# DeltaNet projections in pairs by seven products over half the contraction, first convolution tap on ScalarE

## The chip, the cores and the metric

The kernel runs on one core of a Trainium2 chip. The metric is the device time of one execution in microseconds (us), from the first to the last instruction of the program.

## What is computed

The kernel is a trunk of two layers (DEPTH = 2) over one sequence of 1024 tokens with 1024 channels, all in float32. Each layer normalises its input, projects it by one wide matrix w_in (1024 x 9232), runs two token mixers on the result, a retention with 4 heads and a gated DeltaNet with 8 heads, merges them and adds the layer's output to its input. Of the DeltaNet, which the change is about, this is what has to come out:

```
h = rmsnorm(x, norm_g)
proj = h @ w_in
(rq, rk, rv, rz, dq, dk, dv, dz, db, da, gr, gd) = jnp.split(proj, _split_points(), axis=-1)
qkv = jax.nn.silu(causal_conv(jnp.concatenate([dq, dk, dv], axis=-1), conv_w))   # 4 taps per channel
...
# per head and chunk: a triangular solve, then a recurrence over the chunks
v_new = u_n - w_n @ state
o = q_n @ state + attn_n @ v_new
state = state * exp(gl) + k_n^T @ v_new
...
o_d = rmsnorm(o) * dn_g * silu(dz)
y = sigmoid(gr) * (o_r @ w_up_r) + sigmoid(gd) * (o_d @ w_up_d)
```

## The kernel before

TensorE works in transposed form: a block is 128 columns of w_in (one head's k, q, v or z, or 128 channels of a gate), its result is 128 channels by 1024 tokens, kept as two halves of 512 tokens. A float32 product is made of three products of rounded parts: hi and lo parts of the weights (`w_hi`, `w_lo`) and of the normed input (`act_hi`, `act_lo`, 8 contraction tiles of 128 channels each). `dense_pieces` (L852) yields after every three matmuls (L866, L868, L870); such a **piece** is one contraction tile of one half, so that a block takes 16 pieces and a head's six blocks (K, Z, Q, V and the two gates D and R, of the next head) take 96.

```
eng.matmul(dense_ps[:, to, :], w_hi[:, slot, k, :], hi[:, k, seg], start=(k == 0), stop=False)
eng.matmul(dense_ps[:, to, :], w_hi[:, slot, k, :], lo[:, k, seg], start=False, stop=False)
mm = eng.matmul(dense_ps[:, to, :], w_lo[:, slot, k, :], hi[:, k, seg], start=False, stop=(k == KT - 1))
```

A weight block is loaded by SyncE (`load_w`), rounded to `w_hi` by ScalarE (`split_hi`, 128x1024, L1429) and its rest made by GpSimd as `w_lo` (L2579).

The DeltaNet of a head is cut into an **even** unit (first 512 tokens) and an **odd** unit (last 512 tokens). `unit_schedule(kind)` (L123) is one list of steps for a unit, in 24 slots, and every engine walks this same list in `delta_unit`, does its own part of each step, and waits on semaphores where it needs another engine's. In an even or odd unit each slot is followed by two pieces ("fill"), so 48 pieces fill the gaps of a unit. Each engine takes its steps strictly in order. There is one unit "first" ahead, seven even and seven odd ones in turn, then "even_last" and "odd_last", in each of two layers. The steps that matter below, with their line on each engine (PE is TensorE, DVE VectorE, ACT ScalarE, POOL GpSimd):
- **evac**: ACT copies a finished half block out of PSUM (L1419), which frees the bank for the block after.
- **conv**: four taps on DVE, the first a scaling (L1970), three of multiply-add (L1973), all SBUF to SBUF. **tanh** on ACT (L1435) and **silu** on DVE (L1987) follow.
- **solve**: 15 steps of two small dependent operations on DVE (L2280, L2283), SBUF to SBUF. **spread** (L2290) ends the solve; PE's **level_v 0** (L1141) waits for it. Then **turn 0** (L2237) and the copy L2251 on DVE.
- **ks, xu, so**, once for each of four chunks: PE multiplies the state (ks, L1171), DVE makes u (L2299), PE xu (L1182) waits for u, ACT copies it, PE so (L1195, L1201, L1202), DVE makes the next state (L2314).
- **kt, vs, qt, kq, qe, mask, dec**: transposes, decays and norms, with POOL's squares (L2672), masks (L2659, L2661) and powers (L2666, L2676).
- **z_silu** (L2149): DVE takes the block Z out of PSUM.

## Time and profile before

| | |
|---|---|
| device time, median of 3 runs | 2644.19 us (2643.35 to 2647.51) |
| span of the profiled execution | 2644.2 us |
| PE busy, of the span | 99% (14874 matmuls) |
| DVE busy | 67%; 7 or 8 tenths in the slices of the DeltaNet units |
| ACT busy | 27% |
| POOL busy | 30% |
| granted TensorE clock | 0.999 of full speed |

The profile gives each engine's busy time, the span in slices, the groups of instructions, who waited for whom, and a timeline. For PE an instruction's modelled duration is longer than the distance from one matmul's start to the next, so the price of a matmul is read from starts. The seven pairs of even and odd units of the first layer lie between about 98 and 734 us, those of the second between about 1406 and 2042 us. The profiled execution's span is the device time of one of the runs to 0.1 us, so nothing has to be added around it.

### The profile page before, as it was taken

How to read it: one execution, taken by the hardware profiler on the slowest of the kernel's cores; microseconds unless marked ns; L12 is line 12 of the kernel's file. 1: busy time of each engine (PE TensorE's matmuls, PEld its weight loads, DVE VectorE, ACT ScalarE, POOL GpSimd, SP SyncE). 2: the span in 40 equal slices, each digit the busy share in tenths (PEclk: the TensorE clock that was granted, in tenths of full speed). 3: DMA queues.
4: the chain of work that ended last, by engine and by line, in shares of the span. 5: the costliest groups of instructions: out<-in, count | busy, mean ns of one | idle time of the engine just before them, and what ended most of it. 6: DMA issues, size and time to landing. Idle time of an engine off the chain costs nothing.

```text
span 2644.2 us, 40210 instructions
## 1 busy us (share of the span) xinstructions
PE 2620.6 (99%) x14874; PEld 2238.1 (85%) x14874; DVE 1761.1 (67%) x3972; ACT 704.5 (27%) x1440; POOL 798.6 (30%) x451
## 2 busy tenths in 40 slices
PE   8999999999999999999999999999999999999998
PEld 6888888888888899888877888888888998898887
DVE  7878777877755555434577778777877555653333
ACT  5333333333311212200143333333332221231001
POOL 3123333333312212334512233332322122132453
PEclk9999999999999999999999999999999999999999
DMA  5321222122211112433533222222222111133344
GB/s 174 100 85 58 81 69 85 53 86 65 85 50 43 41 35 76 130 96 120 157 90 88 77 74 69 73 77 72 67 77 73 43 51 43 41 106 100 99 135 152
DMA packets 293416, 217.79 MB, mean 82 GB/s; under 512 B 31747, under 2 KB 246101, under 8 KB 292965
## 3 DMA queue, kind: packets, MB, share of 16 engines
q1 hardware_dynamic: 259620, 159.07, 20.9%
q10 hardware_dynamic: 33600, 56.15, 6.3%
q8 instruction: 119, 1.95, 0.3%
q14 instruction: 77, 0.62, 0.1%
HBM read 176.30 MB, written 38.86 MB: 81 GB/s over the span
## 4 chain that ended last, share of the span: by engine, by line
PE 92%; DVE 3%; DMA 2%; issue 1%; ACT 1%; SPq 0%; POOL 0%; ACTq 0%; DVEq 0%; POOLq 0%
PE dense_ps L866 23%; PE dense_ps L870 23%; PE dense_ps L868 23%; PE work L849 3%; PE dense_ps L890 2%; PE dense_ps L891 2%; PE dense_ps L892 2%; PE work L1145 1%; PE work L1182 1%; PE work L1202 1%; PE work L1121 1%; PE work L1104 1%; PE work L1171 1%; PE work L1195 1%; PE work L1156 1%
## 5 line engine op out<-in xcount | busy, mean ns | idle before, releaser
L866 PE MATMUL dense_ps<-act_hi,w_hi 128*128 128x512 f32 x2552 | 1048.3, 411 | 1.7 <-DVE w_lo L1797 0.8
L870 PE MATMUL dense_ps<-act_hi,w_lo 128*128 128x512 f32 x2552 | 998.4, 391 | 0.0
L868 PE MATMUL dense_ps<-act_lo,w_hi 128*128 128x512 f32 x2552 | 997.3, 391 | 0.0
L2579 POOL TENSOR_TENSOR w_lo<-w_raw,w_hi 128x1024 fp32r<-128x1024 f32 x162 | 400.1, 2470 | 1024.5 <-ACT w_hi L1429 582.7
L870 PEld LDWEIGHTS dense_ps<-act_hi,w_lo 128*128 128x128 f32 x2552 | 479.0, 188 | 105.8
L866 PEld LDWEIGHTS dense_ps<-act_hi,w_hi 128*128 128x128 f32 x2552 | 481.0, 188 | 86.9 <-POOL act_lo L2600 2.3
L868 PEld LDWEIGHTS dense_ps<-act_lo,w_hi 128*128 128x128 f32 x2552 | 481.5, 189 | 78.8 <-issue 0.5
L1973 DVE SCALAR_TENSOR_TENSOR arena<-arena,cols 128x512 f32<-128x512 f32 x288 | 244.3, 848 | 6.1
L1429 ACT ACTIVATE w_hi<-w_raw 128x1024 fp32r<-128x1024 f32 x94 | 99.1, 1054 | 330.5 <-PE dense_ps L870 310.5
L1419 ACT ACTIVATE arena<-dense_ps 128x512 f32<-128x512 f32 x96 | 57.2, 596 | 258.5 <-PE dense_ps L870 258.5
L849 PE MATMUL work<-mk,arena 128*128 128x128 f32 x768 | 112.1, 275 | 7.9 <-DMA arena<-in_x 7.9
L2280 DVE TENSOR_TENSOR arena<-arena 128x60 f32<-128x60 f32 (+14 forms) x480 | 99.9, 208 | 20.2 <-DMA arena<-l_scratch 7.8
L892 PE MATMUL dense_ps<-v_later_lo,act_hi 128*128 128x256 f32 x384 | 107.9, 281 | 0.0
L890 PE MATMUL dense_ps<-v_later_hi,act_hi 128*128 128x256 f32 x384 | 107.9, 281 | 0.0
L891 PE MATMUL dense_ps<-v_later_hi,act_lo 128*128 128x256 f32 x384 | 107.9, 281 | 0.0
L849 PEld LDWEIGHTS work<-mk,arena 128*128 128x128 f32 x768 | 91.8, 142 | 17.7 <-issue 5.2
L2283 DVE TENSOR_TENSOR arena<-arena 128x60 f32<-128x60 f32 (+14 forms) x480 | 92.4, 192 | 16.5
L2666 POOL TENSOR_TENSOR arena<-arena,negh 128x4 f32<-128x4 f32 x32 | 33.0, 1032 | 230.1 <-DVE arena L2180 230.1
L866 PE MATMUL dense_ps<-o_hi,w_hi 128*128 128x512 f32 x256 | 99.6, 389 | 0.0
L868 PE MATMUL dense_ps<-o_lo,w_hi 128*128 128x512 f32 x256 | 99.6, 389 | 0.0
L870 PE MATMUL dense_ps<-o_hi,w_lo 128*128 128x512 f32 x256 | 99.6, 389 | 0.0
L1620 ACT ACTIVATE arena<-work 128x128 f32<-128x128 f32 x128 | 34.9, 273 | 229.7 <-PE work L1182 224.4
(262 smaller groups left out, 4094.7 us busy)
## 6 DMA issues: line engine op xcount, KB each, us to landing
w_raw<-in_w_in SPq DMA_DIRECT2D x138, 512.0 KB, 3.8
arena<-l_scratch SPq DMA_DIRECT2D x64, 256.0 KB
arena<-gate_scratch ACTq DMA_DIRECT2D x64, 256.0 KB, 2.7
gate_scratch<-arena ACTq DMA_DIRECT2D x36, 256.0 KB, 2.0
w_raw<-in_w_out SPq DMA_DIRECT2D x18, 512.0 KB, 3.7
o_scratch<-arena ACTq DMA_DIRECT2D x32, 256.0 KB, 2.2
w_raw<-in_w_up_dn SPq DMA_DIRECT2D x16, 512.0 KB, 3.6
arena<-o_scratch ACTq DMA_DIRECT2D x32, 256.0 KB, 3.7
```

The lines of the kernel that those rows point to most:

```text
L849: mm = eng.transpose(wk[bank][:, c * P:(c + 1) * P], src, ident)
L866: eng.matmul(dense_ps[:, to, :], w_hi[:, slot, k, :], hi[:, k, seg], start=(k == 0), stop=False)
L868: eng.matmul(dense_ps[:, to, :], w_hi[:, slot, k, :], lo[:, k, seg], start=False, stop=False)
L870: mm = eng.matmul(dense_ps[:, to, :], w_lo[:, slot, k, :], hi[:, k, seg], start=False, stop=(k == KT - 1))
L890: eng.matmul(dst, act_hi[:, k, tok], hi[:, k, :], start=(k == 0), stop=False)
L891: eng.matmul(dst, act_lo[:, k, tok], hi[:, k, :], start=False, stop=False)
L892: mm = eng.matmul(dst, act_hi[:, k, tok], lo[:, k, :], start=False, stop=(k == KT - 1))
L1429: eng.activation(w_hi[:, slot, :, :], w_raw[:, :, :], ACT.Copy).then_inc(w_hi_ok.sem, 1)
L1973: eng.scalar_tensor_tensor(out=acc[:, i % 2, :], in0=src, scalar=wcol, in1=acc[:, i % 2, :], op0=ALU.mult, op1=ALU.add).then_inc(conv_s.se ...
L2280: eng.tensor_tensor(xm[:, :, 0:left], column, xs[:, :, k:k + 1].to_broadcast([P, CPH, left]), ALU.mult).then_inc(sv_s.sem, 1)
L2283: eng.tensor_tensor(xs[:, :, k + 1:BASE], xs[:, :, k + 1:BASE], xm[:, :, 0:left], ALU.add)\
L2579: eng.tensor_tensor(w_lo[:, slot, :, :], w_from[second][:, :, :], w_hi[:, slot, :, :].bitcast(F32), ALU.subtract)\
```

## The change

In the even and odd units the six blocks of a head become three **pairs**: K with Z, Q with V, D with R. The contraction tiles 0 to 3 of a pair (the "thin" part: two tiles low, two tiles high, two blocks, two token halves) are a 2 x 2 by 2 x 2 block product and are made by Strassen's scheme in Winograd's form, with seven products of two tiles instead of eight. The tiles 4 to 7 ("J1", "J2") stay as they were. A pair takes 30 pieces instead of 32, and a unit 45 instead of 48.

The seven products need sums of weights (`S1` to `S4`: four GpSimd additions of 128x256 for each pair), nine rounded parts for each pair (ScalarE `part`, seven of 128x256 and two of 128x512, with a GpSimd rest for each), sums of the activations over token halves (`mix`, once in each layer in the unit "first", 14 steps, mostly GpSimd operations of 128x1024), and intermediate results that are carried between three PSUM banks (`p1`, `u3`) or parked in SBUF (`p5`, `u2`) by ScalarE copies. The second token halves of both blocks (`c12`, `c22`) are finished by a VectorE addition from PSUM. The third PSUM bank is `work5`; the products of `level_x` move to `work4`. ScalarE takes the first convolution tap. One product of each pair starts a bank that the pair before has just left: `S1` waits for `c21` to be taken, `S2` for ScalarE's copy of `p1`, and that for `c22` of the pair before.

The late tokens of two activation tiles are replaced by their mix in place; they are stored to DRAM first and loaded back before the unit "even_last". Several semaphores are merged, which changes no order.

```diff
+PARTS = ("X11", "S1", "S2", "X12", "J1", "S3", "S4", "X22", "J2")
+PART_AT = (-14, -12, -9, -6, -3, 3, 5, 7, 10)
+PAIR_PIECES = 30
+UNIT_PIECES = 45
...
+        events = {"p1": 2, "p5": 10 if u % 3 == 1 else 4, "u2": 6, "c11": 12, "u3": 14, "c12": 20, "c21": 26, "c22": 30}
...
+        if paired and waiting and waiting[0][0] == "conv" and waiting[0][2] == 0:
+            out.append(waiting.pop(0))
...
-        for _ in range(2):
+        while paired and pieces < UNIT_PIECES * (n + 1) // len(slots):
+            out.append(("fill", 1))
+            pieces += 1
...
-        elif kind in ("even", "odd"):
-            spread(0 if 3 <= n < 8 or (12 if kind == "even" else 13) <= n < 17 else 2 if n in (12, 17) or n > 17 else 1)
+        elif kind == "even":
+            spread(0 if 3 <= n < 8 or 12 <= n < 17 else 2 if n >= 17 else 1)
+        elif kind == "odd":
+            spread(0 if 3 <= n < 8 or 13 <= n < 17 else 2 if n >= 17 or n in (8, 9, 12) else 1)
...
+                        eng.wait_ge(c12_ok.sem, c12_ok.after(t - 1, 1))
+                        yield from product(t, u, a, "X11", tokens(low_k, early), True, "p1")
...
+                        eng.wait_ge(c21_ok.sem, c21_ok.after(t, 0))
+                        yield from product(t, u, c, "S1", mixed(1), True, "p5")
+                        eng.wait_ge(pc_ok.sem, pc_ok.after(t, COPIES["p1"]))
+                        yield from product(t, u, b, "S2", mixed(2), False, "p6")
+                        yield from product(t, u, a, "X12", tokens(high_k, early))
+                        yield from product(t, u, a, "J1", tokens(rest, early), False, "c11")
+                        eng.wait_ge(pc_ok.sem, pc_ok.after(t, COPIES["u2"]))
+                        yield from product(t, u, b, "S3", mixed(3), False, "p7")
+                        yield from product(t, u, c, "S4", tokens(high_k, late))
+                        yield from product(t, u, c, "J1", tokens(rest, late), False, "c12")
...
+                        eng.wait_ge(pc_ok.sem, pc_ok.after(t, COPIES["u3"]))
+                        yield from product(t, u, b, "X22", mixed(4), False, "p4")
+                        yield from product(t, u, b, "J2", tokens(rest, early), False, "c21")
+                        yield from product(t, u, a, "J2", tokens(rest, late), False, "c22")
...
+                            eng.activation(part_place(part, u, w_hi), part_from[part], ACT.Copy).then_inc(wp_hi.sem, 1)
...
+                        elif what == "conv" and kind in ("even", "odd") and step[2] == 0:
...
+                            eng.activation(acc[:, i % 2, :], raw[:, (i // 2) % 2, i % 2 * HALF:(i % 2 + 1) * HALF], ACT.Copy,
+                                           scale=cols[:, wcol:wcol + 1]).then_inc(conv_s.sem, 1)
...
+                        elif what == "pair" and step[1] in ("c12", "c22"):
...
+                            ins = eng.tensor_tensor(into, of, into, ALU.add)
...
+                            if part == "X11":
+                                eng.wait_ge(wx_in.sem, wx_in.after(w, 32))
+                                eng.tensor_tensor(w_s, raw_x["X21"], raw_x["X22"], ALU.add).then_inc(wp_lo.sem, 1)
+                                eng.wait_ge(wp_lo.sem, wp_lo.after(w, LOWS["sum_S1"]))
+                                eng.tensor_tensor(raw_x["X21"], raw_x["X11"], raw_x["X21"], ALU.subtract).then_inc(wp_lo.sem, 1)
```

What this makes of the order shows at three places. The first is VectorE in an odd unit, from the last solve step to u of the last chunk. Before:

```order
L2283 TENSOR_TENSOR arena<-arena 128x4
L2314 SCALAR_TENSOR_TENSOR arena<-arena,work 128x128
L2290 TENSOR_TENSOR arena<-arena,mk 128x512
L1973 SCALAR_TENSOR_TENSOR arena<-arena,cols 128x512
L2237 STREAM_TRANSPOSE arena<-arena 32x4x32 x4
L2251 TENSOR_TENSOR arena<-work,mk 64x256
L2299 SCALAR_TENSOR_TENSOR arena<-work,arena 128x128
```

And now (L2629 is the solve step, L2468 the addition of c22, L2660 the state, L2636 spread, L2289 a tap, L2645 u):

```order
L2629 TENSOR_TENSOR arena<-arena 128x4
L2468 TENSOR_TENSOR arena<-work,arena 128x512
L2660 SCALAR_TENSOR_TENSOR arena<-arena,work 128x128
L2636 TENSOR_TENSOR arena<-arena,mk 128x512
L2289 SCALAR_TENSOR_TENSOR arena<-arena,cols 128x512 x2
L2583 STREAM_TRANSPOSE arena<-arena 32x4x32 x4
L2597 TENSOR_TENSOR arena<-work,mk 64x256
L2645 SCALAR_TENSOR_TENSOR arena<-work,arena 128x128
```

One addition stands ahead of the spread, and two taps instead of one between spread and u. PE reaches level_v 0 (L1351, L1141 before) one piece after "so" (L1405 to L1412) there, where it had two:

```order
L1405 MATMUL work<-arena 128x128
L1411 MATMUL work<-arena 128x128
L1412 MATMUL work<-arena 128x128
L1218 MATMUL dense_ps<-act_hi,w_hi 128x512
L1219 MATMUL dense_ps<-act_lo,w_hi 128x512
L1220 MATMUL dense_ps<-act_hi,w_lo 128x512
L1351 MATMUL work<-arena 66x64 x4
```

The second place is VectorE from the end of an even unit into the odd one. Before, the last tap pair of the third convolution and its silu stood like this ahead of u of chunk 0 (L2299):

```order
L1970 TENSOR_SCALAR arena<-arena,cols 128x512
L1973 SCALAR_TENSOR_TENSOR arena<-arena,cols 128x512
L1987 SCALAR_TENSOR_TENSOR arena<-arena 128x512
L1973 SCALAR_TENSOR_TENSOR arena<-arena,cols 128x512 x2
L1987 SCALAR_TENSOR_TENSOR arena<-arena 128x512
L2299 SCALAR_TENSOR_TENSOR arena<-work,arena 128x128
```

Now three taps (L2289) stand straight ahead of u (L2645), and the silu (L2303) behind it:

```order
L2573 TENSOR_TENSOR arena<-work,arena 128x512
L2303 SCALAR_TENSOR_TENSOR arena<-arena 128x512
L2289 SCALAR_TENSOR_TENSOR arena<-arena,cols 128x512 x3
L2645 SCALAR_TENSOR_TENSOR arena<-work,arena 128x128
L2303 SCALAR_TENSOR_TENSOR arena<-arena 128x512
```

Their input is `c11` of the pair that started at piece 30 of the even unit: PE finishes it after piece 42 of 45, ScalarE copies it out and makes the first tap, and PE's xu of chunk 0 follows piece 1 of the odd unit (it followed piece 2).

The third place is GpSimd. Before, over one unit:

```order
L2579 TENSOR_TENSOR w_lo<-w_raw,w_hi 128x1024 x2
L2672 TENSOR_TENSOR arena<-arena 128x512
L2579 TENSOR_TENSOR w_lo<-w_raw,w_hi 128x1024
L2659 TENSOR_TENSOR arena<-mk,arena 128x512
L2661 TENSOR_TENSOR arena<-arena,mk 128x512
```

And now, over an odd unit, from the sums of the next pair to J1's rest:

```order
L3051 TENSOR_TENSOR arena<-w_raw 128x256
L3053 TENSOR_TENSOR w_raw<-w_raw 128x256
L3055 TENSOR_TENSOR w_lo<-w_raw,w_hi 128x256
L3060 TENSOR_TENSOR w_raw<-arena,w_raw 128x256
L3055 TENSOR_TENSOR w_lo<-arena,w_hi 128x256
L3055 TENSOR_TENSOR w_lo<-w_raw,w_hi 128x256
L3085 TENSOR_TENSOR arena<-arena 128x512
L3055 TENSOR_TENSOR w_lo<-w_raw,w_hi 128x256
L3064 TENSOR_TENSOR w_raw<-w_raw 128x256
L3055 TENSOR_TENSOR w_lo<-arena,w_hi 128x512
```

The six operations of 128x1024 of a head have become 33 of 128x256 and six of 128x512, and the squares (L3085, L2672 before) and several of the small ones stand at steps that lie inside the solve.

## Rows read from the trace of the kernel before

**Rows 1.** The page: busy time of each engine.

```profile
PE 2620.6 (99%) x14874; PEld 2238.1 (85%) x14874; DVE 1761.1 (67%) x3972; ACT 704.5 (27%) x1440; POOL 798.6 (30%) x451
```

**Rows 2.** Windows: us, busy (instructions) of PE, PEld, DVE, ACT, POOL, clock, DMA, GB/s.

```profile
467.80:556.30 88.50, 88.50 (x523) 75.63 (x522) 71.33 (x182) 29.82 (x65) 27.04 (x16) 1.00 0.25 73
456.80:466.40 9.60, 9.60 (x59) 8.41 (x58) 7.16 (x35) 2.09 (x5) 0.00 (x0) 1.00 0.25 78
```

**Rows 3.** Timeline: start us, us, engine, line, operation; plain blocks, then the even unit's end.

```profile
489.36 0.39 PE L866 MATMUL dense_ps<-act_hi,w_hi 128*128 128x512 f32 x1
489.56 0.60 ACT L1419 ACTIVATE arena<-dense_ps 128x512 f32<-128x512 f32 x1 [4.92 <-PE dense_ps L870]
490.04 0.39 PE L866 MATMUL dense_ps<-act_hi,w_hi 128*128 128x512 f32 x1
...
495.69 0.34 DVE L2299 SCALAR_TENSOR_TENSOR arena<-work,arena 128x128 f32<-128x128 f32 x1
496.41 0.38 PE L1182 MATMUL work<-arena 128*128 128x128 f32 x2
```

**Rows 4.** Timeline, an odd unit, from the solve's end to the last state step.

```profile
510.34 0.38 PE L1195 MATMUL work<-arena 128*128 128x128 f32 x2
...
510.78 0.17 DVE L2283 TENSOR_TENSOR arena<-arena 128x4 f32<-128x4 f32 x1
...
511.22 0.69 DVE L2290 TENSOR_TENSOR arena<-arena,mk 128x512 f32<-128x512 f32 x1
511.82 0.74 DVE L1973 SCALAR_TENSOR_TENSOR arena<-arena,cols 128x512 f32<-128x512 f32 x1
...
512.40 0.64 PE L1141 MATMUL work<-arena 128*66 128x64 f32 x8
...
514.10 0.33 DVE L2299 SCALAR_TENSOR_TENSOR arena<-work,arena 128x128 f32<-128x128 f32 x1
...
514.54 0.43 PE L1182 MATMUL work<-arena 128*128 128x128 f32 x2
```

**Rows 5.** Groups by form over one head, 467.8 to 556.3 us.

```profile
L1973 DVE SCALAR_TENSOR_TENSOR arena<-arena,cols 128x512 f32<-128x512 f32 x18 | 15.5, 864 | 0.4
L1970 DVE TENSOR_SCALAR arena<-arena,cols 128x512 f32<-128x512 f32 x6 | 6.2, 1033 | 0.0
L2329 DVE TENSOR_TENSOR arena<-work,arena 128x512 f32<-128x512 f32 x2 | 1.4, 691 | 0.4 <-POOL arena L2676 0.4
L1419 ACT ACTIVATE arena<-dense_ps 128x512 f32<-128x512 f32 x6 | 3.6, 598 | 17.9 <-PE dense_ps L870 17.9
L2579 POOL TENSOR_TENSOR w_lo<-w_raw,w_hi 128x1024 fp32r<-128x1024 f32 x6 | 14.4, 2399 | 40.9 <-ACT w_hi L1429 40.9
L2672 POOL TENSOR_TENSOR arena<-arena 128x512 f32<-128x512 f32 x2 | 2.6, 1289 | 0.0
...
L2593 POOL TENSOR_TENSOR w_hi<-w_raw,w_hi 128x128 fp32r<-128x128 f32 x1 | 0.5, 459 | 0.0
```

**Rows 6.** Timeline: POOL operations and the DVE operations that start inside them.

```profile
485.51 2.40 POOL L2579 TENSOR_TENSOR w_lo<-w_raw,w_hi 128x1024 fp32r<-128x1024 f32 x1
486.57 1.62 DVE L1970 TENSOR_SCALAR arena<-arena,cols 128x512 f32<-128x512 f32 x1
...
471.95 1.83 DVE L1973 SCALAR_TENSOR_TENSOR arena<-arena,cols 128x512 f32<-128x512 f32 x1
471.97 1.26 POOL L2661 TENSOR_TENSOR arena<-arena,mk 128x512 f32<-128x512 f32 x1
...
101.82 1.29 POOL L2672 TENSOR_TENSOR arena<-arena 128x512 f32<-128x512 f32 x1
102.68 0.52 DVE L2280 TENSOR_TENSOR arena<-arena 128x60 f32<-128x60 f32 x1
```

**Rows 7.** Waits of DVE inside one solve, 456.8 to 466.4 us (timeline).

```profile
462.07 0.35 DVE L2299 SCALAR_TENSOR_TENSOR arena<-work,arena 128x128 f32<-128x128 f32 x1 [0.42 <-PE work L1171]
464.57 0.69 DVE L2223 TENSOR_TENSOR arena<-work,arena 128x512 f32<-128x512 f32 x1 [0.96 <-PE work L1121]
```

539 lines of the change are left out of this document (440 added, 99 removed).

## Prediction

> **What bounds the kernel now.** First the busy shares of the page: PE works 2620.6 of 2644.2 us, DVE 67%, POOL 30%, ACT 27% [rows 1]. The windows over one head of the DeltaNet (one even and one odd unit, here from level_v 0 to level_v 0) show what the page's mean hides: PE is busy in all 88.50 us, DVE in 71.33, POOL in 27.04 [rows 2]. So PE is the bound, and a matmul less is worth its full price as long as nobody else holds PE up. DVE has 17.2 us of idle time in a head, and it is not free time: each engine walks one list in strict order, so what counts is how long before PE needs a result DVE has it. Those margins are small. In the odd unit spread ends at 511.91 and PE reaches level_v 0 at 512.40; u of the last chunk ends at 514.43 and PE's xu stands at 514.54 [rows 4]. The reader should see two margins, of 0.49 and 0.11 us, and that PE has two pieces on each of the two ways.
>
> **What a piece is worth.** The first matmuls of two plain pieces start at 489.36 and 490.04, 0.68 us apart [rows 3]. The change takes 6 pieces from a head, so 84 from 14 heads: 84 x 0.68 = 57.1 us. Two extra matmuls clear a bank, 2 x 0.68/3 = 0.5 us. Left: **-56.6 us**. That is 0.68/3 = 0.227 us for each matmul, with the loads of weights between them. By the Trainium skill ("TensorE: Matmul & The Clock Gate", Part 1) warm matmuls of 512 columns follow each other after 512 / 2.4 GHz plus about 2.5 ns, 216 ns; by that rule the 252 matmuls would give 54.4 us. The row decides, since it holds the weight loads.
>
> **DVE's own work.** Of a head, six first taps leave it: 6 x 1.033 = 6.2 us. Six additions from PSUM come, priced as L2329, 0.691: 4.1 us [rows 5]. Net -2.1 us, against 4.1 us that PE gives up in a head. ACT gains at most 12 copies, 6 taps and 27 casts; at the 0.60 us of a 128x512 copy [rows 5], which is above what 21 casts of half the size should take, that is 27 us on top of 29.82 in 88.50 [rows 2], before the casts and copies that it loses. It stays idle a third of the time or more; what it can cost is only its place in a chain. The DMAs carry the same bytes in 12 loads of 256 KB for a head instead of six of 512; they are asked for nine pieces or more ahead and cost nothing. The stored and reloaded late tokens (4 DMAs a layer) and the rope table lie under even and odd units: nothing, or a few us of wait ahead of "even_last" if they are late.
>
> **The waits that the new order makes.** Here the term is read as margin before, less what is put in front of it, less the pieces taken from PE's way.
> - Odd unit, level_v 0. Before, the solve ended 0.61 us after PE's "so" (510.34 to 510.95), spread at +1.57, PE at +2.06 [rows 4]. Now the addition of c22 stands in front of spread (+0.69), and one piece less, about 0.70, lies on PE's way. PE at +1.36, DVE at +2.26: **0.9 us**.
> - Odd unit, xu of the last chunk. Between spread and u there is a second tap, 0.74 [rows 4]; the two pieces stay. Before, u was ready 2.52 us after spread (511.91 to 514.43), and PE stood there 2.14 after it began level_v 0; now PE begins level_v 0 when spread ends, and it is 3.26 against 2.14: **1.1 us**.
> - Odd unit, xu of chunk 0. ACT copies c11 0.2 us after PE's piece 42 begins the next (489.56 against 489.36) [rows 3], 0.60 for the copy, as much for the first tap, three taps of 0.74, u 0.34: 4.0 us. PE has three pieces, ks (some 0.15) and one more piece: 2.9 us. **1.1 us**, where the margin had been 0.4 (496.41 less 496.03) [rows 3].
> - Even unit, by the odd unit's rows: level_v 0 loses a piece but gets no addition, 0.70 - 0.49 = 0.2; xu of its last chunk has one tap, 2.52 - 2.14 = 0.35 with the wait for the semaphore. S1 and S2 of the next pair have four to six pieces and find their banks nearly free: nothing.
> Sum 3.65 a head, x 14 = **+51 us**. These are additive as far as each is counted from the step before it, where PE and DVE are level again.
>
> **What POOL does to DVE.** The rows of POOL beside DVE [rows 6] hold what I take for the costliest point. A first tap that starts at 486.57 inside a POOL operation ends at 488.19, 0.28 after that ends (487.91); a tap started at 471.95 ends at 473.78, 0.55 after POOL's 473.23; a solve step that starts at 102.68 takes 0.52 us and ends just after POOL's 103.11; the whole solve of 30 such steps and more lasts 9.6 us [rows 2], so a step has 0.2 or 0.3. A DVE operation with two SBUF inputs (or a fast single one) waits for the whole POOL operation. The Trainium skill says as much in kind ("GPSIMD Engine Reference", 8. Key points: POOL shares its SBUF interfaces with VectorE and collides with two-input operations), not that the wait lasts as long as the operation; the rows agree and add that. Today POOL does nothing at all during a solve: 0.00 in 456.80 to 466.40 [rows 2]. Now POOL's own work grows from 14.4 us of rests for a head to 33 operations of 128x256 and six of 128x512. The trace has no 256; between 0.459 at 128 and 1.289 at 512 [rows 5] it is 0.74, so 24.4 + 7.9 = 32 us. Of these stand in a solve: in the even unit X22's rest, the squares, J2's rest and two sums, 0.74 + 1.29 + 1.35 + 1.48 = 4.9 us; in the odd unit S2, the squares, X12 with a sum, J1, 4.9 as well. A solve has 0.42 + 0.96 us of idle time to hide them [rows 7]. So the price lies between 0 (they fall where DVE reads PSUM) and (9.8 - 2.8) = 7 us a head. I take the middle, since POOL starts each when ACT's cast is done and the solve is a gapless chain but not the only work there: 3.5 x 14 = **+49 us**. Collisions with taps cost 15.5 - 18 x 0.74 = 2.2 us a head now [rows 4, 5] and may grow by 1 or 2; they end in the same margins and lie in the range.
>
> **The first unit.** Thirteen POOL operations of 2.4 us [rows 5] are put there, 31 us, in a unit of 64 pieces (44 us and its own steps), of which a part is over when the first can start. PE needs the mixes at piece 3 of the first even unit. Taken at nothing; up to 12 us a layer if POOL is late.
>
> **Sum.** 2644.2 - 56.6 + 51 + 49 = 2687.6, **2688 us** forecast, 1.6% slower. The execution profiled and the median of the runs shown (2644.19) are the same to 0.1 us.
>
> **Rivals.**
> - *The waits are hidden, full gain.* The place is the stretch from the solve to xu in the odd unit. It needs DVE to arrive there at least 3.1 us earlier against PE's pieces than now. For it: DVE's work falls by 2.1 us a head, and it idles 17.2. Against it: the idle time lies where DVE waits for PE (462.07, 464.57) [rows 7], and in the end of the odd unit, not ahead of these steps. The point from which it decides is 56.6/14 = 4.0 us of waits a head: below it the kernel is faster. With all hidden: 2644.2 - 56.6 = 2588 us. With the waits of the order at half and POOL's at a quarter of its upper bound: 2644.2 - 56.6 + 26 + 25 = 2639.
> - *Even.* The waits of the order come, POOL's falls into gaps: 2644.2 - 56.6 + 51 = 2639, at the edge of no change; with a fraction of POOL's, 2640 to 2650.
> - *DVE becomes the bound.* POOL's whole 7 us a head hit the solve, and the taps lose 1.5 more: 2644.2 - 56.6 + 51 + 119 = 2758, and with late mixes up to 2782. For it: a solve is 30 small operations one after the other, each of which needs the last, so a POOL operation in the solve is always met.
> - *The change does not do what it says*: fewer pieces is plain in the order (14624 matmuls against 14874), so this has no chance of its own.
>
> **How the numbers follow.** About 0.2% (5 us) is what a measurement of this kernel can tell from no change. Forecast case (2655 to 2725) 0.36, DVE-bound case above it 0.20; hidden 0.34, with times between 2588 and 2639; even 0.10 (0.08 inside 5 us, 0.02 above). Faster 0.34, same 0.08, slower 0.58. The range leaves the lowest tenth (full gain to the last us) and the highest tenth out: 2592 to 2762. The slower cases' own range is 2655 to 2762.
>
> **What would show it.** Right: pieces still 0.68 us apart, PE idle or stretched in front of level_v 0 (L1351) and of xu (L1392) with DVE's spread (L2636) and u (L2645) as releasers, 1 us each in odd units; solve steps (L2626, L2629) with means well above 0.3 us and POOL busy above 50% in the solve; a head of 91.6 us (2688 less 2644 over 14 heads is 3.1 more than 88.5). Wrong: a head of 84.4 us with PE busy throughout (full gain), solve steps at their old means (POOL's term falls), or waits of PE mainly on pair_copies or wp_lo (ACT or POOL late by themselves, which I count at nothing).

## The result: 2877 us, 8.8% slower, and where the time went

The changed kernel takes 2876.99 us (median of 4 runs, 2875.95 to 2880.9) against 2643.8 before: a ratio of 1.0879 (95% interval 1.0864 to 1.0894). The forecast was 2688 with 2762 as its upper end, so the side was right and the size was off by a factor of five: 233 us slower, not 44.

The page after, as [rows 1] of before:

```profile
PE 2641.8 (92%) x14624; PEld 2204.7 (77%) x14624; DVE 1900.3 (66%) x3970; ACT 893.6 (31%) x1952; POOL 1184.1 (41%) x943
```

250 matmuls fewer, and yet 21 us more busy time of PE: a part of them ran at a lower clock (0.984 of full speed over the span where it was 0.999, some 43 us), and single matmuls between waits lie further apart. Windows over one head, then the solves of its even and its odd unit, as [rows 2] (us, then busy time and instructions of PE, PEld, DVE, ACT, POOL, clock, DMA share, GB/s):

```profile
496.90:599.70 102.80, 90.22 (x504) 73.75 (x504) 77.47 (x182) 42.84 (x100) 48.79 (x49) 0.97 0.23 63
529.63:541.77 12.14, 10.23 (x60) 8.37 (x58) 10.96 (x34) 4.82 (x11) 5.39 (x7) 1.00 0.34 102
585.99:597.79 11.80, 9.99 (x59) 8.20 (x57) 10.61 (x35) 3.34 (x8) 4.71 (x5) 1.00 0.10 24
```

The head takes 102.8 us in place of 88.5, a solve 12 in place of 9.6, and POOL is busy 5 us in each solve in place of none. DVE's busy time of the head rose by 6 us: single operations of it take longer than before.

The waits of PE in the whole kernel (line, who released it: us in total, times, longest):

```profile
PE work L1392 <- DVE arena L2645: 56.0, 72, 1.1
PE work L1405 <- ACT arena L1938: 44.4, 14, 4.4
PE work L1381 <- DVE arena L2660: 36.7, 28, 1.8
PE work L1351 <- DVE arena L2636: 33.3, 30, 7.4
PE work L999 <- DVE arena L2303: 17.6, 4, 8.5
PE work L1381 <- DVE arena L2655: 9.2, 2, 5.8
```

These are xu behind u, "so" behind ScalarE's copy of v_new, ks behind the state update, level_v 0 behind spread, the token turns of the unit "first" behind a silu, and ks of "even_last" behind the state copy.

Laid side by side from one start of level_v 0 to the next, the two traces give this ledger. Behind the plus sign stands what the pieces saved (0.68 us each) would have taken off:

| stretch | times | before | after | longer, + pieces | = waits |
|---|---|---|---|---|---|
| to the first level_v 0 of a layer (the second counted from the last one of the first layer) | 2 | 77.9, 649.4 | 97.5, 670.1 | 40.3 + 0 | 40 |
| "first" to the first even unit | 2 | 36.0, 39.1 | 40.9, 40.8 | 6.6 + 2.7 | 9 |
| even to odd unit | 14 | 44.6 | 51.9 to 56.7 | 135.2 + 28.6 | 164 |
| odd to even unit | 12 | 43.9 | 46.1 | 26.5 + 24.5 | 51 |
| last odd to "even_last" | 2 | 43.9 | 55.4, 54.3 | 21.9 + 1.4 | 23 |

The sum is 230.5 us longer, of a difference of spans of 231.2; 288 us of waits and slow clock against 57 us of pieces. Over the whole span PE's idle time rose from 23.6 to 233.6 us, 210 of the 288; some 43 are the clock, by an estimate from its mean, and the other 35 or so, by difference, lie between matmuls that follow each other more slowly at full clock. The largest line is 164 / 14 = 11.7 us a head. The prediction had 4.1 there: 0.35 for xu of the even unit's last chunk, 1.1 and 0.9 in the odd unit, and half of POOL's 3.5. "Odd to even" costs 4.25 where 1.1 + 0.2 + 1.75 = 3.05 was forecast.

**One such stretch.** SyncE, ScalarE, PE and GpSimd of it on the timeline (start us, us, engine, line, operation, idle time before and its releaser):

```profile
563.95 3.62 SPq L846 DMA_DIRECT2D l_scratch<-arena  x8
569.43 1.22 SPq L854 DMA_DIRECT2D arena<-l_scratch  x2
570.69 1.01 SPq L870 DMA_DIRECT2D w_raw<-in_w_in  x2
...
573.52 0.38 PE L1392 MATMUL work<-arena 128*128 128x128 f32 x1 [1.11 <-DVE arena L2645]
...
578.63 0.42 ACT L1779 ACTIVATE w_hi<-w_raw 128x256 fp32r<-128x256 f32 x1 [7.06 <-DMA w_raw<-in_w_in]
578.95 0.61 ACT L1645 ACTIVATE arena<-arena 128x512 f32<-128x512 f32 x1
579.47 0.26 ACT L1938 ACTIVATE arena<-work 128x128 f32<-128x128 f32 x1
...
579.78 0.80 PE L1405 MATMUL work<-arena 128*128 128x128 f32 x2 [4.38 <-ACT arena L1938]
```

The raw block of the next pair is asked for at 570.7, behind the store and reload of the level blocks, and lands 7.9 us later. ScalarE stands 7.06 us at its cast; the copy of v_new (L1938), for which PE's xu was done soon after 573.5, is two places behind it in the list; PE stands 4.38 us. The 14 waits of this kind are 2.0 to 4.4 us long. Then the clock:

```profile
580.00:585.50 5.50, 5.50 (x20) 4.82 (x21) 2.39 (x5) 0.55 (x2) 2.76 (x4) 0.50 0.00 0
```

Granted clock 0.50, which is 1.2 GHz of the two levels, for 5.5 us right after PE had been idle 4.4 us: by an estimate another 2.75 us. It is not so behind each of these waits, and their length does not decide it: behind one of 2.97 us it was 0.50, behind one of 3.51 us 1.00. In the 5.5 us behind the 14 waits at "so" the granted clock is 0.50 twice, 0.55 once, 0.69 or 0.70 six times and 1.00 five times; the sum of what is missing to 1.00, times 5.5, is 18 us. In the kernel before the clock was 0.999 over the span.

By the Trainium skill ("TensorE: Matmul & The Clock Gate", Part 1) the gate lets pass either half or all of the clock's pulses, by how busy the array has been; the trace agrees: cut into half microseconds, a stretch of 5.5 us with 0.70 (from 681.2 us) reads 0.50 up to 684.2, 0.70 once, and 1.00 from 684.7 on. So a value between 0.50 and 1.00 is a stretch that holds some of both.

In the solve that follows, POOL's operations and VectorE's steps, as [rows 6]:

```profile
588.66 0.73 POOL L3055 TENSOR_TENSOR w_lo<-w_raw,w_hi 128x256 fp32r<-128x256 f32 x1
...
592.46 1.29 POOL L3055 TENSOR_TENSOR w_lo<-arena,w_hi 128x512 fp32r<-128x512 f32 x1 [2.25 <-ACT w_hi L1779]
...
588.81 0.65 DVE L2629 TENSOR_TENSOR arena<-arena 128x52 f32<-128x52 f32 x1
590.31 0.21 DVE L2629 TENSOR_TENSOR arena<-arena 128x48 f32<-128x48 f32 x1
591.49 0.35 DVE L2660 SCALAR_TENSOR_TENSOR arena<-arena,work 128x128 f32<-128x128 f32 x1
592.47 1.33 DVE L2629 TENSOR_TENSOR arena<-arena 128x32 f32<-128x32 f32 x1
```

A step takes 0.21 us when POOL is idle, 0.65 inside an operation of 0.73 and 1.33 inside one of 1.29. The steps of a solve add up to 9.5 to 9.9 us where they had 6.0. Line L2660 is the state update for which ks 2 waits: it stands in this list behind twelve steps.

**The unit "first".** Groups of VectorE, after (60 to 97.5 us), and the same line before (50 to 77.9), then PE's two waits:

```profile
L2289 DVE SCALAR_TENSOR_TENSOR arena<-arena,cols 128x512 f32<-128x512 f32 x3 | 8.6, 2880 | 0.0
L2303 DVE SCALAR_TENSOR_TENSOR arena<-arena 128x512 f32<-128x512 f32 x2 | 5.7, 2858 | 0.0
```

```profile
L1973 DVE SCALAR_TENSOR_TENSOR arena<-arena,cols 128x512 f32<-128x512 f32 x8 | 6.0, 749 | 0.1
```

```profile
72.50 0.48 PE L999 MATMUL work<-mk,arena 128*128 128x128 f32 x1 [8.39 <-DVE arena L2303]
...
97.53 0.38 PE L1351 MATMUL work<-arena 128*66 128x64 f32 x1 [7.41 <-DVE arena L2636]
```

A tap costs 2.88 us instead of 0.75, since each meets one of POOL's 14 mixes of 2.4 to 3.3 us, as here:

```profile
71.97 2.73 POOL L2987 TENSOR_TENSOR arena<-act_hi,arena 128x1024 f32<-128x1024 f32 x1
72.37 2.88 DVE L2289 SCALAR_TENSOR_TENSOR arena<-arena,cols 128x512 f32<-128x512 f32 x1
```

### The profile page after: what moved, and what is told of

Read it like the earlier page. It is cut to its first block, busy times and chain, and to the rows that moved or that the text cites. A ratio compares the mean times of both kernels' runs of the same rounds, so it can differ in the third digit from the quotient of the medians.

```text
span 2875.4 us, 41656 instructions
## 1 busy us (share of the span) xinstructions
PE 2641.8 (92%) x14624; PEld 2204.7 (77%) x14624; DVE 1900.3 (66%) x3970; ACT 893.6 (31%) x1952; POOL 1184.1 (41%) x943
## 4 chain that ended last, share of the span: by engine, by line
PE 56%; DVE 14%; issue 10%; POOL 7%; DMA 7%; SPq 3%; ACT 2%; ACTq 0%; DVEq 0%; POOLq 0%
PE dense_ps L1016 10%; PE dense_ps L1018 10%; PE dense_ps L1020 10%; DMA w_raw<-in_w_in 5%; POOL w_lo L3055 3%; DVE arena L2626 3%; PE dense_ps L1218 2%; PE dense_ps L1219 2%; PE dense_ps L1220 2%; PE dense_ps L1040 2%; PE dense_ps L1041 2%; PE dense_ps L1042 2%; DVE arena L2629 2%; SPq L846 2%; PE work L999 2%
## 5 line engine op out<-in xcount | busy, mean ns | idle before, releaser
L1016 PE MATMUL dense_ps<-act_hi,w_hi 128*128 128x512 f32 x1208 | 486.9, 403 | 8.8 <-POOL w_lo L2925 4.5
L1020 PE MATMUL dense_ps<-act_hi,w_lo 128*128 128x512 f32 x1208 | 474.9, 393 | 0.0
L1018 PE MATMUL dense_ps<-act_lo,w_hi 128*128 128x512 f32 x1208 | 474.8, 393 | 0.0
L3055 POOL TENSOR_TENSOR w_lo<-w_raw,w_hi 128x256 fp32r<-128x256 f32 x252 | 226.2, 901 | 439.1 <-ACT w_hi L1779 439.1
L2925 POOL TENSOR_TENSOR w_lo<-w_raw,w_hi 128x1024 fp32r<-128x1024 f32 x80 | 203.3, 2541 | 466.9 <-DVE w_hi L2107 444.7
L2289 DVE SCALAR_TENSOR_TENSOR arena<-arena,cols 128x512 f32<-128x512 f32 x288 | 273.6, 950 | 49.0 <-ACT arena L1798 41.6
L1218 PE MATMUL dense_ps<-act_hi,w_hi 128*128 128x512 f32 x672 | 290.7, 433 | 0.0
L1219 PE MATMUL dense_ps<-act_lo,w_hi 128*128 128x512 f32 x672 | 267.4, 398 | 0.0
L1020 PEld LDWEIGHTS dense_ps<-act_hi,w_lo 128*128 128x128 f32 x1208 | 229.0, 190 | 50.1
L1220 PE MATMUL dense_ps<-act_hi,w_lo 128*128 128x512 f32 x672 | 266.7, 397 | 0.0
L1018 PEld LDWEIGHTS dense_ps<-act_lo,w_hi 128*128 128x128 f32 x1208 | 229.7, 190 | 42.0 <-issue 0.5
L3055 POOL TENSOR_TENSOR w_lo<-arena,w_hi 128x512 fp32r<-128x512 f32 (+1 forms) x126 | 146.7, 1164 | 56.8 <-ACT w_hi L1779 56.8
L1220 PEld LDWEIGHTS dense_ps<-act_hi,w_lo 128*128 128x128 f32 x672 | 128.5, 191 | 29.1
L1219 PEld LDWEIGHTS dense_ps<-act_lo,w_hi 128*128 128x128 f32 x672 | 129.7, 193 | 17.7
L2629 DVE TENSOR_TENSOR arena<-arena 128x60 f32<-128x60 f32 (+14 forms) x480 | 130.7, 272 | 16.5
L2303 DVE SCALAR_TENSOR_TENSOR arena<-arena 128x512 f32<-128x512 f32 x96 | 93.1, 970 | 72.2 <-ACT arena L1645 70.1
L1218 PE MATMUL work<-act_hi,w_hi 128*128 128x512 f32 x336 | 139.9, 416 | 0.0
L1220 PE MATMUL work<-act_hi,w_lo 128*128 128x512 f32 x336 | 131.8, 392 | 0.0
```

The costliest lines, as they stand in the source:

```text
L1218: eng.matmul(bank, hi[:, k, :], acts[0][:, k, :], start=first, stop=False, skip_group_check=True)
L1219: eng.matmul(bank, hi[:, k, :], acts[1][:, k, :], start=False, stop=False, skip_group_check=True)
L1220: mm = eng.matmul(bank, lo[:, k, :], acts[0][:, k, :], start=False, stop=last, skip_group_check=True)
L2289: eng.scalar_tensor_tensor(out=acc[:, i % 2, :], in0=src, scalar=wcol, in1=acc[:, i % 2, :], op0=ALU.mult, op1=ALU.add).then_inc(conv_s.se ...
L2629: eng.tensor_tensor(xs[:, :, k + 1:BASE], xs[:, :, k + 1:BASE], xm[:, :, 0:left], ALU.add)\
L2925: eng.tensor_tensor(w_lo[:, slot, :, :], w_from[second][:, :, :], w_hi[:, slot, :, :].bitcast(F32), ALU.subtract)\
```

## The experiments

Each is an edit of the changed kernel, except experiment 4, and is given as its time and the ratio to the kernel before with its 95% interval.

### 1. The cast behind the copy

```diff
-PART_AT = (-14, -12, -9, -6, -3, 3, 5, 7, 10)
+PART_AT = (-11, -10, -8, -6, -3, 3, 5, 7, 10)
```

> The changed kernel with the places of the weight parts of the next pair moved: X11 from 14 pieces ahead of its pair to 11, S1 from 12 to 10, S2 from 9 to 8. Theory: once a head ScalarE stands 6.7 us at the cast of X11 in front of the transfer of the raw block (it lands 7.5 us after its issue), the copy of v_new for 'so' of chunk 0 is queued behind that cast, so TensorE stands 4.2 us at 'so', and then runs some 5 us with its pitch at 0.43 instead of 0.23 us. With the cast three pieces later the copy is ahead of it: 14 x (4.2 + 2.5 to 3) = 94 to 100 us less than the changed kernel, some 2780 us. Rival: the wait only moves, to the products of the next pair (TensorE waits for the parts on GpSimd): then 20 us or less come back, 2857 or more.

Measured 2838.43 us (1.0711 to 1.0743): 38.5 less, not 97 and not nothing. The wait at "so" is gone, but the one at ks 2 grew from 36.7 to 61.3 us. PE, and one window over a solve of this run:

```profile
PE work L1381 <- DVE arena L2660: 61.3, 28, 3.8
```

```profile
566.95:581.62 14.67, 11.09 (x55) 9.11 (x54) 11.89 (x35) 3.50 (x8) 7.00 (x9) 0.88 0.08 20
```

Most of the sums and the first rests now fall into the solve: POOL is busy 7.0 us in it where it had been 4.7, the solve lasts 14.7 us in place of 11.8, and the granted clock over it is 0.88. The block that held ScalarE up now holds VectorE up.

### 2. The mixes in smaller operations

```diff
-eng.tensor_tensor(out, in0, in1, op).then_inc(mx_ok.sem, 1)
+for k in range(2):
+    for q in range(2):
+        at = slice(256 * q, 256 * q + 256)
+        ins = eng.tensor_tensor(out[:, k, at], in0[:, k, at], in1[:, k, at], op)
+ins.then_inc(mx_ok.sem, 1)
```

> The changed kernel with each of the 13 GpSimd operations of 128x1024 on the token mixes of a layer written as four of 128x256. Theory: in the unit 'first' VectorE's taps last 2.8 us instead of 0.75 since each waits for the whole GpSimd operation of 2.7 us that it meets; with operations of 0.7 us a tap waits at most 0.7, some 20 to 24 such VectorE operations in the two layers get 1.5 to 2 us shorter each, and of the two waits of TensorE of 8.8 and 7.8 us a layer at least half goes: 15 to 35 us less, 2842 to 2862. Rival: what costs there is GpSimd's whole work of 31 us (VectorE waits as long in total whatever the size): no change within 3 us.

Measured 2880.01 us (1.0862 to 1.0898): no gain; the median is 3 us higher, and the time that the rival forecast came. A tap now takes 1.2 us instead of 2.9, but there are more operations of POOL left when the solve comes, and its steps take 0.55 us instead of 0.2:

```profile
L2629 DVE TENSOR_TENSOR arena<-arena 128x60 f32<-128x60 f32 (+14 forms) x15 | 8.5, 565 | 0.5
...
L2289 DVE SCALAR_TENSOR_TENSOR arena<-arena,cols 128x512 f32<-128x512 f32 x3 | 3.6, 1212 | 0.0
```

So the delay of one tap does go by the length of the operation that it meets, and what was saved there was lost again behind it. That POOL's total alone decides is not shown, since the total did not stay: the 28 mixes of both layers take POOL 75.0 us in one piece each and 90.1 us in quarters.

### 3. POOL's weight operations in the solves cut to 8 columns (computation left out)

```diff
-eng.tensor_tensor(part_place(part, u, w_lo), part_from[part], ...)
+cut = slice(0, 8 if few else P)
+eng.tensor_tensor(part_place(part, u, w_lo)[:, :, cut], part_from[part][:, :, cut], ...)
```

> The changed kernel, but from the second head of each layer on the GpSimd rests and the sum whose turn falls into a solve (S4, X22, J2 of the first pair of a head and S2, X12, J1 of the third) are done over 8 of 128 columns; the other columns of those weight rests keep old values, so this leaves computation out. Theory: the solve's own steps rose from 6.0 to 9.4 (even to odd) and 9.9 us since each step that meets a GpSimd operation waits for its end; without them the steps fall to some 7 us or less, 5 us a head come off VectorE's chain, and TensorE's waits ahead of ks 2, xu 2 and level_v 0 (6.1 us a head now) fall by 3 to 5 us: 12 heads x 3 to 5 = 36 to 60 us less, 2817 to 2841. Rival: these waits come from the order alone (c22's addition ahead of spread): 10 us or less.

Measured 2827.26 us (1.0664 to 1.0695): 49.7 less, 4.1 us for each of the 12 heads in which the operations are cut. The solves, an odd and an even unit's:

```profile
472.32:481.75 9.43, 9.43 (x59) 8.29 (x57) 8.02 (x35) 3.34 (x8) 2.16 (x5) 1.00 0.12 30
516.46:526.19 9.73, 9.73 (x60) 8.53 (x58) 8.82 (x34) 4.71 (x11) 3.51 (x7) 1.00 0.44 130
```

They are back at 9.4 and 9.7 us, with PE busy throughout, and the wait for L2660 (36.7 us) is no longer among PE's larger ones. The wait at "so" stays, 40.9 us.

### 4. Half the change alone: the first tap on ScalarE

```diff
+elif what == "conv" and kind in ("even", "odd") and step[2] == 0:
+    ...
+    eng.activation(acc[:, i % 2, :], raw[...], ACT.Copy, scale=cols[:, wcol:wcol + 1]).then_inc(conv_s.sem, 1)
```

> The kernel before with only the second part of the change: the first tap of each convolution in even and odd units as a scaled copy on ScalarE, at the place where it stood. Theory: VectorE loses 6.2 us of work a head, but TensorE is the bound and ScalarE has 59 us of idle time a head: 2644 within 3 us. Rival: the copy stands in ScalarE's list ahead of copies for which TensorE waits, 0.6 us each: up to 14 x 2 = 28 us more.

Measured 2647.0 us against 2645.15 of the kernel before (0.9999 to 1.0018): no change. 24 us of VectorE's busy time less, and the end stays where PE puts it. That is 1.7 us a head, not the 6.2 of the six first taps in [rows 5]: over the same head the 18 other taps (L1983 here) got longer, 19.7 us in place of 15.5, since they now meet the GpSimd operations that the first taps had met.

```profile
L1983 DVE SCALAR_TENSOR_TENSOR arena<-arena,cols 128x512 f32<-128x512 f32 x18 | 19.7, 1093 | 3.1 <-ACT arena L1564 2.7
```

### 5. The weights first on SyncE

```diff
-                    l_blocks(2 * h + 2, 0)
                     pair_load(3 * h + 2, None)
+                    l_blocks(2 * h + 2, 0)
```

> The changed kernel with one step of SyncE's list moved: the load of the third pair's raw blocks ahead of the store and reload of the level blocks of the even unit. Theory: the raw block is late because it is asked for at 367.1, behind the store (360.3 to 364.8) and the reload, though its buffer is free at 364.9, and then shares the DMA engines with the reload (7.5 us to land); asked for first it lands 2 to 4 us earlier, so ScalarE's wait of 5.8 us in each head and TensorE's 4.2 us at 'so' shrink by as much: 14 x (2 to 4) = 28 to 56 us less and some of the 14 slow-clock stretches go: 2790 to 2850. Rival: the buffer and the transfer itself set it, and the level blocks then come late to the next solve: no gain, or slower by 1 to 3 us a head, 2877 to 2920.

Measured 2854.09 us (1.0772 to 1.0804): 22.9 less. The block is asked for at 359.8 and ScalarE casts it at 363.6, 3.8 us later instead of 7.5 in the same head of the changed kernel (367.1 to 374.6):

```profile
359.81 0.92 SPq L870 DMA_DIRECT2D w_raw<-in_w_in  x2
360.83 3.73 SPq L846 DMA_DIRECT2D l_scratch<-arena  x8
...
363.62 0.42 ACT L1779 ACTIVATE w_hi<-w_raw 128x256 fp32r<-128x256 f32 x1 [0.85 <-DMA w_raw<-in_w_in]
```

```profile
PE work L1381 <- DVE arena L2660: 63.4, 28, 3.9
```

ScalarE's waits for this block fall from 81.8 to 13.0 us, PE's wait at "so" is gone, and again it comes back at ks 2. So the lateness was made on SyncE's queue, by the place behind the level blocks: there the block was asked for 2.2 us after its buffer had come free (367.1 after 364.9), here at once (359.8), and from issue to cast it took 3.7 us longer right behind their reload.

### 6. Experiments 1 and 3 together

> The first and the third experiment together: X11 at 11, S1 at 10, S2 at 8 pieces ahead, and the GpSimd rests and the sum in the solves over 8 of 128 columns (computation left out, as there). Alone they gave 38.5 and 50 us. Theory: with the parts later the GpSimd work of X11 falls onto the first nine steps of the odd unit's solve, each step waits for it, and the state update of chunk 1, queued behind them on VectorE, makes TensorE wait 3.8 us at ks 2, so the two costs stand in for each other; but the thin variant still has X11's own rest and its three sums (2.9 us) there, so part of it stays: ks 2's wait falls to 1 to 2.5 us and the sum is 110 to 130 us, 2747 to 2767. Rival: they simply add to 88 us: 2788.

Measured 2772.53 us (1.0462 to 1.0496): 104.5 less, more than the 88 of the two alone and less than the 110 of the theory. The two costs hide each other in part, for 16 us.

### 7. The other half undone: the first tap back on VectorE

```diff
-elif what == "conv" and (step[2] or kind == "first"):
+elif what == "conv":
```

> The changed kernel with its second part undone: the first taps of even and odd units on VectorE at the same places. Theory: VectorE gets six operations of 0.35 to 1.03 us a head back; of the places where TensorE waits for it only u of chunk 0 of the odd unit (behind the four taps of c11) has a first tap in front, and there ScalarE's copy of 0.72 us is replaced by a tap of 0.35 us or more without the wait between the engines: within 10 us of 2877 either way, and ScalarE's queue is no cause of the loss. Rival: VectorE's total work is what costs: 14 x 4 = 50 us or more slower.

Measured 2890.78 us (1.0908 to 1.094): 13.8 slower, between the two. Not the place that I had named but level_v of the later levels got a wait: `level_v 1` behind a late step of VectorE, 14.0 us in 14 waits, 1 us a head. In the changed kernel VectorE is idle 0.5 us in the 9 us ahead of that step (from 603 to 612), so the tap on ScalarE earns 1 us a head, which it could not do in experiment 4. The expectation, within 10 us, was missed.

### 8. Four moves in the order

```diff
-PART_AT = (-14, -12, -9, -6, -3, 3, 5, 7, 10)
+PART_AT = (-13, -12, -9, -6, -3, 3, 5, 7, 10)
...
+        if u % 3 == 1:
+            events["c22"] = 31
...
-            spread(0 if 3 <= n < 8 or 12 <= n < 17 else 2 if n >= 17 else 1)
+            spread(0 if 3 <= n < 9 or 12 <= n < 17 else 2 if n >= 17 or n == 9 else 1)
```

with the swap of experiment 5, and the like for the odd unit.

> The changed kernel with four moves and the whole computation: the raw blocks first on SyncE as in experiment 5; X11 one piece later, so that ScalarE copies v_new first; the addition of c22 of the second pair after spread instead of ahead of it; and no taps between spread and u of the last chunk (they follow behind it). Theory: TensorE's waits ahead of level_v 0 in the odd unit (1.2 us), of xu 3 (1.1 and 0.8 us) and at 'so' (4.2 us and the slow clock behind it) go or fall below 0.5 us each, and those of ks 2 and xu 0 stay: 14 x (2.5 to 3) + 14 x (4 to 6) = 91 to 126 us less than the changed kernel, 2751 to 2786. Rival: VectorE's chain is late as a whole, and what is taken away at one place comes back at ks 2 or level_x: 40 us less at most, 2837 or more.

Measured 2843.18 us (1.0731 to 1.0763): 33.8 less, of which experiment 5 alone gives 22.9. The rival holds for the rest:

```profile
PE work L1394 <- DVE arena L2647: 36.6, 45, 1.7
PE work L1357 <- DVE arena L2615: 23.6, 14, 1.7
...
PE work L1353 <- DVE arena L2638: 16.1, 17, 5.9
```

xu fell from 56.0 to 36.6 us and level_v 0 from 33.3 to 16.1, as meant, and level_v 1 (L1357), which had no wait, got 23.6: the taps moved behind u now stand in front of it. The largest wait, 64.3 us at ks 2, is that of experiment 5. Odd to even went from 46.1 to 47.3 us a head, so the moves of taps lost there a part of what they gave.

### 9. The operations of the solves on VectorE itself

```diff
+ON_DVE = {0: ("S4", "X22", "J2"), 1: (), 2: ("S2", "X12", "J1")}
...
+elif what == "part" and step[1] in ON_DVE[step[2] % 3]:
+    ...
+    eng.tensor_tensor(part_place(part, u, w_lo), part_from[part], ..., ALU.subtract).then_inc(wp_lo.sem, 1)
```

> The changed kernel with the whole computation, but the seven weight operations of a head whose turn falls into a solve (S4, X22, J2; S2, X12 with its sum, J1) on VectorE in place of GpSimd. Theory: a GpSimd operation of 0.74 us in the solve holds VectorE up for some 0.5 us and one of 1.3 for 1.0, since it waits for the end; VectorE itself would need about 0.35 for 128x256 and 0.7 for 128x512, 3.3 us a head against 5 us of waits: 1 to 2 us a head less, 14 to 28 us, 2849 to 2863. Rival: VectorE now waits in its solve for ScalarE's casts and for the transfer, and that costs more than the waits on GpSimd: slower than 2877 by 10 us or more.

Measured 2833.1 us (1.069 to 1.0722): 43.9 less, more than expected, with nothing left out. A solve of an odd unit:

```profile
472.41:481.78 9.37, 9.37 (x58) 8.18 (x57) 8.48 (x39) 3.35 (x8) 0.00 (x0) 1.00 0.05 11
```

VectorE does the four operations itself and the solve is still 2.4 us shorter than with POOL's help; an even unit's takes 10.5 in place of 12.1. Not all of that is the move itself: POOL's squares (L3102, L3085 in the changed kernel), which had been stuck behind the rest of S2 and so fell into the odd unit's solve, are now done 0.9 us ahead of it:

```profile
470.27 1.27 POOL L3102 TENSOR_TENSOR arena<-arena 128x512 f32<-128x512 f32 x1
486.90 0.72 POOL L3072 TENSOR_TENSOR w_lo<-w_raw,w_hi 128x256 fp32r<-128x256 f32 x1 [15.36 <-ACT w_hi L1780]
```

The wait at ks 2 is gone, and level_v 0 waits 51.9 us where it had 33.3.

### 10. The mixes on VectorE itself

The function that makes the mixes is called from VectorE's list in place of POOL's.

> The changed kernel with the whole computation, but the 13 token mixes of a layer on VectorE in place of GpSimd, at the same places. Theory: in the unit 'first' VectorE and GpSimd take turns: each of some 13 two-input operations of VectorE is lengthened by 2.1 us (27 us a layer) by GpSimd's 31 us. VectorE does a mix in about 1.4 us, 18 us for 13: the unit gets 5 to 9 us shorter in each layer, 10 to 18 us less, 2859 to 2867. Rival: VectorE is busy nearly all the time there anyway, so its sum of work decides and it is the same or more: no gain, or slower by up to 10 us.

Measured 2858.4 us (1.0781 to 1.0819): 18.6 less. The first level_v 0 comes at 85.3 us instead of 97.5 (77.9 before the change), of which 3.4 us are lost again in the next stretch. A mix takes VectorE 1.22 us, half of POOL's time.

### 11 and 12. Everything mended, and then without the operands' price

Experiment 11 joins experiments 8, 9 and 10, and adds two moves:

```diff
-elif what == "qt":
+elif what == ("qt" if kind == "first" else "qe"):
...
+order.remove(("so", 1))
+order.insert(order.index(("solve", 4)), ("so", 1))
```

> Whole computation. The four moves of experiment 8, the weight operations in the solves and the mixes on VectorE (experiments 9 and 10), GpSimd's product for the decayed q after the solve, and VectorE's state update of chunk 1 ahead of solve step 4 in place of step 6. Theory: the wait ahead of ks 2 (3.4 us in the odd unit and 1.5 in the even) falls below 1 us each, since no step ahead of it in the list waits for GpSimd: 2843 less 14 x (3 to 4.5) less 10 to 15 for the mixes: 2765 to 2790, still slower than the kernel before. Rival: VectorE's list as a whole is behind, and the wait moves to level_v and xu: 2820 or more.

Measured 2806.04 us (1.0588 to 1.0619): 71.0 less than the changed kernel, in between. The waits for the state update at ks 2 are gone (what ks still waits, 10.4 us, is the state copy at the end of a layer), but level_v 0, level_v 1 and xu still wait 37.1, 26.3 and 43.3 us.

> Experiment 11 with every weight rest and weight sum of the pairs, on GpSimd and on VectorE, over 8 of 128 columns from the second head of each layer on (computation left out: those columns keep old values). It takes away the whole price of making Strassen's operands in 12 of 14 heads and leaves the order of the lists, the additions from PSUM, ScalarE's casts and the first units. Theory: the waits left in experiment 11 (xu 3.1 us, level_v 2.7 and 1.9 us a head) come partly from this work; 3 to 5 us a head go: 2806 less 36 to 60, 2746 to 2770, so that the order and the first units alone still eat the 57 us of pieces and some 110 more. Rival: the operands are the whole trouble and without them the kernel is near 2644 less 57 plus the first units' 20 to 40: 2610 to 2650.

Measured 2716.77 us (1.0261 to 1.0295): 89.3 less again, more than the theory's 60 and far from the rival. One head of it:

```profile
444.80:534.10 89.30, 85.85 (x504) 71.67 (x504) 67.48 (x189) 42.86 (x100) 21.72 (x42) 1.00 0.26 72
```

Even with nearly free operands a head takes 89.3 us, 0.8 more than the 88.5 of the kernel before, though it has 504 matmuls for 523; six pieces fewer would be 84.4. So of the 162 us that experiment 11 is above the kernel before, the work of making the operands on POOL and VectorE is the larger part (89 us in 12 heads). What is left in such a head, 4.9 us, still eats the 4.1 that the pieces give: there PE waits for u, level_v 1 and level_v 0. The shorter cover for the chain of the DeltaNet is one reason; the additions from PSUM, ScalarE's casts and copies and the order of the lists are still there too, and no run takes them apart. The trace is 67 us above the kernel before, and 50 of these lie outside the seven even and odd pairs of a layer, by the ledger's stretches: 14 up to the first level_v 0, 12 from "first" to the even unit, 24 ahead of "even_last".

### 13 and 14. The last unit of a layer

In the changed kernel the trace puts 11.78 us of VectorE's idle time there on a weight block:

```profile
839.23 0.69 DVE L2107 CAST w_hi<-w_raw 128x1024 fp32r<-128x1024 f32 x1 [11.78 <-DMA w_raw<-in_w_in]
839.84 0.28 DVE L2655 COPY arena<-work 128x128 f32<-128x128 f32 x1
...
840.27 0.55 PE L1381 MATMUL work<-arena 128*128 128x128 f32 x1 [5.79 <-DVE arena L2655]
```

but VectorE also waits there for the rope table, 1 MB, 12.2 us from issue to landing. Experiment 13 issues the table later and waits for it where it is used:

```diff
-eng.wait_ge(rope_in.sem, rope_in.after(l, 16))
 delta_unit("even_last", DH - 1)
...
+if kind == "even_last" and c == 1:
+    eng.dma_start(rope_t, ...).then_inc(rope_in.sem, 16)
```

> The changed kernel with the rope table's load (1 MB) issued by ScalarE in the unit 'even_last' at its second 'xu' step, not at 'restore' at the end of the last odd unit, and VectorE's wait for it moved from the start of 'even_last' to the first rope step. Theory: the unit with 'restore' takes 55.4 instead of 43.9 us in both layers because VectorE, which has the state copy that TensorE needs at ks 1 in its list, waits there 11.8 us for this table (12.2 us from issue to landing, beside the weight block); without it TensorE's wait of 5.8 us and the slow clock behind it go: 2 x (7 to 10) = 14 to 20 us less, 2857 to 2863. Rival: the late tokens (four transfers) or the weight block of the same time are what is late, and the wait stays: within 4 us of 2877.

Measured 2873.68 us (1.0852 to 1.0888): 3.3 less, hardly more than the runs of one kernel differ. The two units take 51.8 and 52.6 us instead of 55.4 and 54.3; PE's waits for the state copy fall from 9.2 to 6.3 us in the two layers, and the larger part of VectorE's wait stays:

```profile
831.16 0.69 DVE L2108 CAST w_hi<-w_raw 128x1024 fp32r<-128x1024 f32 x1 [8.43 <-DMA w_raw<-in_w_in]
```

It is probably both: with the table out of the way the block comes sooner, but the block itself, issued behind the level blocks and a gate store (823.8) and landed 7.3 us later, is late by itself, beside the late tokens that come back at the same time. How much those tokens add was not tried.

> Experiment 11 with the move of experiment 13, and one tap fewer beside slot 12 of the odd unit; whole computation. Theory: the gains add, 2806 less 14 to 22: 2784 to 2792, the shortest form of this change that computes all, and still 5% slower than the kernel before. Rival: in experiment 11 the last unit's wait is hidden behind others: 2800 or more.

Measured 2796.54 us (1.0562 to 1.0593): 9.5 below experiment 11, between theory and rival; one tap fewer beside slot 12 is in it as well, so the table's part alone is not shown. The shortest form with the whole computation is 152 us slower than the kernel before.

## Why the prediction was wrong in size, point by point

- **A piece's price, -56.6 us: right.** Two plain pieces of the changed kernel are as far apart as in [rows 3], 0.68 us:

```profile
362.16 0.39 PE L1218 MATMUL work<-act_hi,w_hi 128*128 128x512 f32 x1
...
362.84 0.39 PE L1218 MATMUL work<-act_hi,w_hi 128*128 128x512 f32 x1
```

- **DVE's own work: mis-sized, with the wrong sign.** The sum took 6.2 us a head off for the first taps and put 4.1 on for the additions. Their 1.033 us hold waits on POOL, which stay when the tap goes: experiment 4 takes off 1.7 us a head, experiment 7 puts 3.0 back (42.4 us of busy time). So with 4.1 us of additions VectorE got more to do, not 2.1 us less. Experiment 4 shows the move at nothing on the end of the kernel before.
- **ScalarE: right on the amount, wrong on the place.** "It stays idle a third of the time or more; what it can cost is only its place in a chain" was the sentence to follow up: the place in the chain, a cast ahead of the copy of v_new, cost 2.0 to 4.4 us of waiting in each of 14 heads, 44.4 in all.
- **"They are asked for nine pieces or more ahead and cost nothing": the step that failed.** Nine pieces are 6.1 us; the block took 7.5 to 7.9 us from issue to use in the two heads shown, and its issue itself was 2 us late behind the level blocks (its buffer was free at 364.9, it was asked for at 367.1). PE waited 44.4 us at "so", and the slow clock behind nine of the 14 waits is 18 more: together an estimated 62 us where the sum had none. Experiments 1 and 5 remove it and get only 38.5 and 22.9 back, since the state update behind the locked solve is next in line.
- **The waits that the new order makes: right in place and nearly in size.** In the head shown, level_v 0 of the odd unit waited 1.04 (forecast 0.9), xu of its last chunk 0.97 (1.1), xu of chunk 0 1.11 (1.1), the even unit 0.29 and 0.65 (0.2 and 0.35): 4.1 us against 3.65. That ks 2 would wait was missed; it is the place where VectorE's list has the state update behind twelve solve steps.
- **What POOL does to DVE: the mechanism right, the value at the bound.** The solve's steps rose by 3.5 and 3.9 us, 7.4 a head, where 3.5 was taken and 7 was the bound. On the end of the kernel its part in the solves weighs 49.7 us (experiment 3), and 104.5 less 38.5 = 66 once the transfer is out of the way (experiments 6 and 1).
- **"The first unit. Taken at nothing; up to 12 us a layer": failed by more than its bound.** It costs 20 us a layer. The same lock that was worked out for the solve was not applied to the mixes (14, not 13), three times as long, beside taps that are all two-input operations. Experiment 10 gets 18.6 of the 40 back.
- **The last unit** was left at "nothing, or a few us": 23 us in both layers, by transfers again.
- **The rival "DVE becomes the bound", 2758 to 2782,** named the right mechanism and is 95 us short: the transfer and the clock behind it, and the first and last units, are what it did not hold.

The sum had 100 us of waits (51 and 49), the ledger has 288. Of the 188 missing, 62 are the block's lateness, 40 the first unit and 23 the last. The runs and the trace place these of the 288: 62 at "so" and its clock, 40 in "first", 23 in the last units, 14 x 4.1 = 57 by the order, 36.7 at ks 2. The remaining 69 were not taken apart by a run; the trace shows in them xu 2 behind ks 2 (0.76 us in the odd unit shown), 9 us between "first" and the first even unit, and a part of the 35 us or so between matmuls at full clock.

## What to carry to other kernels

Fewer matmuls also mean less cover (the ledger's odd to even stretch, 4.25 us of waits for 3 pieces less): each piece taken from between two steps of a chain on other engines must be paid for with the same microseconds of margin there, so look for those margins before counting the pieces. Price every load by its queue: what stands ahead of it on the issuing engine, when its one buffer comes free, how long it lands beside others, and who else is queued behind the engine that waits for it. And work that GpSimd does beside two-input VectorE operations isn't free help: here it was quicker to let VectorE do it itself (experiments 9 and 10).
